# Prompt attention of a hybrid decoder step: two heads of each key group per unit, one fp32 copy of the probabilities, row scaling on GpSimd

## The reference

```python
def nsa_attend(q, gts, q_pos, k_cmp, v_cmp, k_sel, v_sel, k_win, v_win, win_pos, rel_bias):
    qs = q * (HEAD_DIM ** -0.5)
    ...
    lg = jnp.einsum('bqghd,bngd->bghqn', qs, k_cmp) + tab[t5_bucket(d_cmp)].transpose(2, 3, 0, 1)
    p_cmp = masked_softmax(lg, m_cmp)
    o_cmp = jnp.einsum('bghqn,bngd->bqghd', p_cmp.astype(v_cmp.dtype), v_cmp)
    ...
    o_sel = jnp.einsum('bghqnk,bgqnkd->bqghd', p_sel.reshape(shp).astype(vs.dtype), vs)
    ...
    o_win = jnp.einsum('bghqw,bwgd->bqghd', p_win.astype(v_win.dtype), v_win)
    g = jax.nn.sigmoid(gts.astype(jnp.float32)).astype(q.dtype)[..., None]
    return g[:, :, 0] * o_cmp + g[:, :, 1] * o_sel + g[:, :, 2] * o_win
```

## Time and profile before

| | |
|---|---|
| median of 3 runs | 1977.09 us (1969.35 to 1984.14) |
| span of the profiled execution | 1956.9 us |
| what lies between its span and the median | 20.2 us |
| prompt attention, first transpose to last fold | 616.65 us |
| TensorE, VectorE, ScalarE, GpSimd busy in that stretch | 551.09, 491.77, 448.30, 0.00 us |

### The profile page before, as it was taken

How to read it: one execution, slowest core, us unless ns; L and a number is a source line. 1 busy time by engine, 2 the same in 40 slices (tenths; PEclk the granted TensorE clock), 3 DMA queues, 4 the chain that set the end, 5 groups by cost and what they waited for, 6 DMA issues and landing times.

```text
span 1956.9 us, 25523 instructions
## 1 busy us (share of the span) xinstructions
PE 1734.6 (89%) x9736; PEld 1455.2 (74%) x9736; DVE 922.1 (47%) x1784; ACT 734.6 (38%) x1443; POOL 96.0 (5%) x156
## 2 busy tenths in 40 slices
PE   5798999999999998996889988998898758879996
PEld 1387999999999997664777777777677535568883
DVE  0443222221221222345887887787787645533321
ACT  0132111111111112435677777777777523232110
POOL 1003000000000002100000000000000000000000
PEclk9899999999999999988899999999999969889998
DMA  6419533233233225621002100100100164433320
GB/s 235 142 44 160 166 88 77 75 76 87 66 76 87 66 54 206 213 82 52 12 22 50 33 22 23 44 22 22 33 23 22 55 221 155 135 107 111 108 73 17
DMA packets 166924, 164.66 MB, mean 84 GB/s; under 512 B 48322, under 2 KB 143170, under 8 KB 162507
## 3 DMA queue, kind: packets, MB, share of 16 engines
q1 hardware_dynamic: 152100, 93.49, 17.6%
q0 software_dynamic: 14704, 69.53, 11.3%
HBM read 131.32 MB, written 35.83 MB: 85 GB/s over the span
## 4 chain that ended last, share of the span: by engine, by line
PE 75%; DVE 8%; ACT 6%; DMA 5%; issue 4%; SPq 0%; DVEq 0%; POOL 0%; ACTq 0%
PE PS L749 28%; PE PS L1034 9%; PE PS L786 4%; PE PS L877 4%; PE PS L865 3%; DVE ptl L1555 3%; PE PS L837 3%; PE PS L838 3%; ACT pth L1187 2%; PE PS L878 2%; PE PS L1000 2%; DMA adaw<-in_ada_w 2%; PE PS L967 2%; PE PS L885 2%; DMA wr<-in_w_in 2%
## 5 line engine op out<-in xcount | busy, mean ns | idle before, releaser
L749 PE MATMUL PS<-hhi,wh 128*128 128x352 f32 x1152 | 251.4, 326 | 10.5 <-DVE wl L1386 6.9
L749 PE MATMUL PS<-hhi,wl 128*128 128x352 f32 x1152 | 249.5, 324 | 0.0
L749 PE MATMUL PS<-hlo,wh 128*128 128x352 f32 x1152 | 249.3, 325 | 0.0
L1187 ACT ACTIVATE pth<-PS 128x512 fp32r<-128x512 f32 x296 | 176.9, 597 | 140.8 <-PE PS L865 139.0
L1510 DVE TENSOR_REDUCE nm<-PS 128x1 f32<-128x640 f32 (+7 forms) x256 | 180.4, 705 | 77.7 <-PE PS L845 75.5
L1555 DVE TENSOR_TENSOR ptl<-PS,pth 128x512 fp32r<-128x512 f32 x296 | 203.5, 688 | 26.3 <-ACT pth L1187 19.3
L749 PEld LDWEIGHTS PS<-hhi,wh 128*128 128x128 f32 x1152 | 197.1, 190 | 11.7 <-issue 11.2
L749 PEld LDWEIGHTS PS<-hhi,wl 128*128 128x128 f32 x1152 | 199.0, 189 | 0.0
L749 PEld LDWEIGHTS PS<-hlo,wh 128*128 128x128 f32 x1152 | 196.8, 189 | 0.0
L1170 ACT ACTIVATE pr<-PS,nm 128x640 f32<-128x640 f32 (+7 forms) x256 | 178.4, 697 | 30.4 <-DVE nm L1510 29.8
L865 PE MATMUL PS<-ident,pr 128*128 128x128 f32 x1056 | 158.9, 273 | 0.0
(11 more groups left out here) (297 smaller groups left out, 2844.0 us busy)
## 6 DMA issues: line engine op xcount, KB each, us to landing
wr<-in_w_in SPq DMA_DIRECT2D x32, 512.0 KB, 4.4
adaw<-in_ada_w SPq DMA_DIRECT2D x6, 2048.0 KB, 8.6
wr<-in_w_in SPq DMA_DIRECT2D x32, 256.0 KB, 3.5
qb<-q_stacked SPq DMA_DIRECT2D x32, 256.0 KB, 3.5
mr<-mixed SPq DMA_DIRECT2D x16, 512.0 KB, 3.8
mixed<-ych POOLq DMA_DIRECT2D x8, 528.0 KB, 3.3
z_attn_silu<-zab POOLq DMA_DIRECT2D x8, 528.0 KB, 3.0
xb<-in_x_prompt POOLq DMA_DIRECT2D x8, 512.0 KB, 3.8
```

Of the source, the lines that this page charges most:

```text
L749: ins = pe.matmul(PS[:, bank + c, 0:CH], a[kind % 2][:, k, :], b[:, k, c * CH:(c + 1) * CH], start=(k == 0 and b is hhi and a is wh), stop ...
L1187: act.activation(pth[tc % 2][:, :], PS[:, 4 + tc % 2, :], ACT.Copy).then_inc(pt_hi, 1)
```

## The change

A unit is now two heads of each key group (heads 2jp, 2jp+1 of both groups) for one query tile, still 4 heads. The transposed probabilities are copied once, in fp32, into one of six buffers (pt): even tiles by ScalarE, odd tiles by VectorE (copy_p). The products with the values are plain fp32, two for each tile: one for each key group, with 64 columns of stationary values and 256 of moving probabilities, one into partitions 0 to 63 of the output bank, the other into 64 to 127. The output bank alternates between 6 and 7; the fold (osb, reduce_o) is gone, and the split copies of the values as well. TensorE keeps the tiles in a list (held) and does the products of four or five tiles in a row. All four heads' rows are scaled on GpSimd. The query tensor is stored in the new order of heads; DMAs keep their number and sizes.

```diff
 
-ACT_A, ACT_B = {0, 1}, {0, 1}
+NPT5 = 6
...
-        osb = sb("osb", [P, 512], cx=c4)
-        zau = [sb(f"zau{i}", [P, 4, P], cx=c4) for i in range(2)]
-        mixs = [sb(f"mixs{i}", [P, 4, P], cx=c4) for i in range(2)]
+        pt = [sb(f"ptt{i}", [P, 4, P], cx=c4) for i in range(NPT5)]
+        zau = [sb(f"zau{i}", [P, 2, P], cx=c4) for i in range(2)]
+        mixs = [sb(f"mixs{i}", [P, 2, P], cx=c4) for i in range(2)]
...
         def unit(u):
-            return u // 16, u // 8 % 2, TILE_ORDER[u % 8]
+            return u // 8, TILE_ORDER[u % 8]
+
+        def head_of(u, h):
+            return 8 * (h // 2) + 2 * (u // 8) + h % 2
+
+        def pairs(t):
+            return t.rearrange("p (g j) -> p g j", g=NG)
 
         def tiles_of(w):
-            i = unit(w // 2)[2]
+            i = unit(w // 2)[1]
...
             cuts = [(n * q + 2) // 4 for q in range(5)]
             return [range(cuts[q], cuts[q + 1]) for q in range(4)]
+
+        def turned(c):
+
+            return (pt_dve if c % 2 else pt_act), c // 2 + 1
...
+
+            def scale(w):
+                k, r = keys_of(w)[0], w % 3
+                po.wait_ge(r_rdy, w + 1)
+                for h in range(4):
+                    ins = po.tensor_scalar(pr[r][:, h, 0:k], pr[r][:, h, 0:k], rg[:, r, h:h + 1], None, ALU.mult)
+                ins.then_inc(n_pool, 1)
+
             for b in range(NB):
                 if b == 1:
+                    for w in range(NI):
+                        scale(w)
                     po.wait_ge(r_ev, NU)
                     po.wait_ge(pv_mm, tile0[NI])
...
+                        pe.wait_ge(n_dve, w // 2 + 1)
                 if tc >= 2:
-                    pe.wait_ge(pt_hi, tc - 1)
-                    pe.wait_ge(pt_lo, tc - 1)
+                    pe.wait_ge(*turned(tc - 2))
                 for h in range(4):
                     cmp_ = w % 2 and t == tiles_of(w) - 1
...
             def values(w, t):
                 tc, u = tile0[w] + t, w // 2
-                g, hs, i = unit(u)
-                pe.wait_ge(pt_hi, tc + 1)
-                pe.wait_ge(pt_lo, tc + 1)
+                i = unit(u)[1]
+                pe.wait_ge(*turned(tc))
                 first, last = w % 2 == 0 and t == 0, w % 2 == 1 and t == tiles_of(w) - 1
-                if first and u:
-                    pe.wait_ge(o_ev, u)
-                v = vsx[:, t, g, :] if w % 2 == 0 else vcp[:, g, :] if last else vwx[:, max(0, i - 4) + t, g, :]
-                pe.matmul(PS[:, 6, :], v, pth[tc % 2][:, :], start=first, stop=False)
-                pe.matmul(PS[:, 6, :], v, ptl[tc % 2][:, :], start=False, stop=last).then_inc(pv_mm, 1)
-
-            def reduce_o(u):
-                g = unit(u)[0]
-                pe.wait_ge(o_ev, u + 1)
-                if u:
-                    pe.wait_ge(r_ev, u)
-                pe.matmul(PS[64 * g:64 * g + 64, 7, :], stack2[:, :], osb[:, :], start=True, stop=True).then_inc(r_mm, 1)
-
-            pe.wait_ge(vb_hi, 5)
-            pe.wait_ge(vb_lo, 3)
+                if first and u >= 2:
+                    pe.wait_ge(r_ev, u - 1)
+                for g in range(NG):
+                    if last:
+                        v = vcp[:, g, :]
+                    elif w % 2:
+                        v = kvt[:, max(0, i - 4) + t, C_VW + HD * g:C_VW + HD * g + HD]
+                    else:
+                        v = kvt[:, t, C_VS + HD * g:C_VS + HD * g + HD]
+                    ins = pe.matmul(PS[64 * g:64 * g + 64, 6 + u % 2, 0:2 * P], v, pt[tc % NPT5][:, 2 * g:2 * g + 2, :].rearrange("p j c -> p (j c)"), start=first, stop=last)
+                ins.then_inc(pv_mm, 1)
+
...
                 for h in range(4):
...
             for w in range(NI):
                 for h, part in enumerate(slots(w)):
-                    for t in part or [None]:
-                        if t in (None, part.start) and w + 2 < NI:
-                            scores(w + 2, h)
-                        if t is not None:
-                            turn_p(w, t)
-                        if t is not None:
-                            if behind:
-                                values(*behind)
-                            behind = (w, t)
-                    if h == 2 and w % 2 == 0 and w:
-                        reduce_o(w // 2 - 1)
-            values(*behind)
-            reduce_o(NU - 1)
+                    if w + 2 < NI:
+                        scores(w + 2, h)
+                    for t in part:
+                        turn_p(w, t)
+                        held.append((w, t))
+                    old = [x for x in held if x[0] < w - w % 2] if h == 2 else []
+                    go = max(len(old), len(held) - 1 if len(held) >= 5 else 0)
+                    for x in held[:go]:
+                        values(*x)
+                    held = held[go:]
+            for x in held:
+                values(*x)
...
 
-            def scale(w):
-                act.wait_ge(r_rdy, w + 1)
-                for h in sorted(ON_ACT[w % 2]):
-                    k, r = keys_of(w)[0], w % 3
-                    ins = act.activation(pr[r][:, h, 0:k], pr[r][:, h, 0:k], ACT.Copy, scale=rg[:, r, h:h + 1])
-                ins.then_inc(n_act, 1)
-
-            def high(w, t):
+            def copy_p(w, t):
                 tc = tile0[w] + t
                 act.wait_ge(t_mm, tc + 1)
-                if tc >= 2:
-                    act.wait_ge(pv_mm, tc - 1)
-                act.activation(pth[tc % 2][:, :], PS[:, 4 + tc % 2, :], ACT.Copy).then_inc(pt_hi, 1)
-
-            def sums(u):
-                act.wait_ge(pv_mm, tile0[2 * u + 2])
-                if u:
...
                 for h, part in enumerate(slots(w)):
-                    for t in part or [None]:
-                        if t in (None, part.start):
-                            if ahead:
-                                exps(*ahead)
-                            ahead = (w + 2, h) if w + 2 < NI else None
-                        if t is not None:
-                            high(w, t)
-                            if behind is not None:
-                                sums(behind)
-                                behind = None
-                    if w + 1 < NI and h == 2:
-                        scale(w + 1)
-                if w % 2:
-                    behind = w // 2
-            sums(NU - 1)
-            act.wait_ge(r_mm, NU)
+                    for t in part:
+                        if (tile0[w] + t) % 2 == 0:
+                            copy_p(w, t)
+                    if w + 2 < NI:
...
+                    dve.tensor_tensor(prc[r][:, :, 0:2 * i + 2], prc[r][:, :, 0:2 * i + 2], ext(rg[:, r, 4:8], (0, 2 * i + 2)), ALU.mult).then_inc(n_dve, 1)
+
+            def copy_p(w, t):
                 tc = tile0[w] + t
-                dve.wait_ge(pt_hi, tc + 1)
-                if tc >= 2:
-                    dve.wait_ge(pv_mm, tc - 1)
-                dve.tensor_tensor(ptl[tc % 2][:, :], PS[:, 4 + tc % 2, :], f32(pth[tc % 2][:, :]), ALU.subtract).then_inc(pt_lo, 1)
+                dve.wait_ge(t_mm, tc + 1)
+                if tc >= NPT5:
+                    dve.wait_ge(pv_mm, tc - NPT5 + 1)
+                dve.tensor_copy(pt[tc % NPT5][:, :, :], PS[:, 4 + tc % 2, :].rearrange("p (h c) -> p h c", h=4)).then_inc(pt_dve, 1)
 
             def gate_o(u):
-                g, hs, i = unit(u)
-                half = slice(64 * g, 64 * g + 64)
-                dve.wait_ge(r_mm, u + 1)
+                dve.wait_ge(pv_mm, tile0[2 * u + 2])
                 dve.wait_ge(za_ld[u % 2], 16 * (u // 2 + 1))
                 if u >= 2:
                     dve.wait_ge(mix_st[u % 2], 16 * (u // 2))
-                dve.tensor_tensor(mixs[u % 2][half, :, :], PS[half, 7, :].rearrange("p (j c) -> p j c", j=4), zau[u % 2][half, :, :], ALU.mult).then_inc(r_ev, 1)
+                dve.tensor_tensor(mixs[u % 2][:, :, :], PS[:, 6 + u % 2, 0:2 * P].rearrange("p (j c) -> p j c", j=2), zau[u % 2][:, :, :], ALU.mult).then_inc(r_ev, 1)
 
...
-                        if t is not None:
-                            if behind:
-                                low(*behind)
-                            behind = (w, t)
-                        if t in (None, part.start) and w + 2 < NI:
-                            maxima(w + 2, h)
-                    if w + 1 < NI:
-                        if h == 1:
-                            factors(w + 1)
-                        for hh in ((), (0, 1), (2, 3), ())[h]:
-                            scale(w + 1, hh)
+                    if w + 2 < NI:
+                        maxima(w + 2, h)
+                    for t in part:
+                        if (tile0[w] + t) % 2:
+                            copy_p(w, t)
+                    if w + 1 < NI and h == 1:
+                        factors(w + 1)
                     if h == 3 and w % 2 == 0 and w:
                         gate_o(w // 2 - 1)
-            low(*behind)
             gate_o(NU - 1)
```

152 lines of the change are left out of this document (63 added, 89 removed).

## The result

The kernel with the change takes 2076.19 us (median of 4 runs, 2061.09 to 2093.7), the kernel before 1973.22 in the same comparison (4 runs, 1967.61 to 1984.14). The ratio is 1.0555, with a 95% interval of 1.0497 to 1.0612: slower by 103 us, where 86 us less was forecast.

What follows compares the result with a forecast made beforehand. No engine was full in attention; TensorE waited 27.5 of 154.5 us a repeat, in lock step with the copies. Stage -92, GpSimd's delay +8, edges -2 made -86 us: 1977 to 1891, forecast 1890 us, range 1862 to 1955.

Steps and rivals of the forecast that it cites:

- the price of a column on GpSimd: Row scaling in attention: 1.1 ns a column, taken nearest to GpSimd's fills; 172 us in sum, hidden.
- My upper bound of 2.6 ns: GpSimd's scaling: reading, multiplying and writing each take a fill's time for a column.
- 4.9 us were needed and 4.7 free: Before 1024 keys: GpSimd's four rows need 4.9 us; TensorE's other work less VectorE's lag leaves 4.7.
- 2 us in a repeat, 8 in all: Attention stage: loss from GpSimd's scaling being 0.5 to 1 us late in a few short iterations.
- GpSimd sets the pace: Rival: GpSimd's scaling at 1.5 to 2.6 ns a column delays transposes; 1915 to 2010 us, middle 1940; chance 0.16.
- The value products: TensorE in attention: two fp32 halves run side by side, 0.43 us a tile, 31.8 us a repeat.
- two halves in series: Rival: a tile's two value products run one after another, 0.85 us instead of 0.43; 1991 us; chance 0.06.
- The change of shape: TensorE's switch of array shape around each block of value products: 0.3 us, 20 blocks and 6 us a repeat.
- mostly go: Attention: the 91 us of the products' waiting for ptl and pth should mostly vanish with the single copy.
- the waiting stays: Rival: waiting may only move from the products to the transposes; 1945 us; chance 0.12.
- The four short iterations: Four shortest iterations of a repeat: 25.4 us before, 16.5 of TensorE's work; taken as 21 after.
- The sum: Whole kernel: -92 us attention stage, +8 GpSimd's delay, -2 edges, making -86 us.

Runs made afterwards that it cites:

- The probe: The kernel before with GpSimd instructions on scratch tiles during the large projection, four forms at three sizes; multiplying 1024 columns by a per-row scalar took 2851 ns.
- two-and-two kernel: The changed kernel with row scaling taken off GpSimd, heads 0 and 1 on ScalarE, 2 and 3 on VectorE, in slot 1: 1883.62 us, ratio 0.9575.
- Three kernels with the same instructions on TensorE: The changed kernel (2076.19 us), it with factors made in slot 0 instead of 1 (1957.43 us), and it with GpSimd's scaling as a product of two tensors (1914.31 us).
- factors in slot 0, two and two: The two-and-two kernel with the factors and VectorE's scaled rows moved to slot 0 from slot 1: 1921.46 us, ratio 0.9781.
- groups apart: The two-and-two kernel with a block's value products ordered as all of key group 0 first, then all of group 1: 1958.35 us, ratio 0.9936.
- smaller blocks: The two-and-two kernel with value products one tile behind their transposes, 219 blocks instead of 79: 1920.26 us, ratio 0.9806; with three of six buffers 1924.7 us.
- three-engine split: The changed kernel with scaling of head 0 on ScalarE, 1 and 2 on VectorE, 3 on GpSimd: 1889.65 us, ratio 0.9595.
- one row to three: The two-and-two kernel with scaling of one row on ScalarE and three on VectorE instead: 1898.59 us, ratio 0.9651.
- product form: The changed kernel with GpSimd's scaling written as a product of two tensors, the factor repeated along the row: 1914.31 us, ratio 0.9765.

## Why the prediction was wrong

**The step that failed** is the price of a column on GpSimd: 1.1 ns and 0.09 us an instruction, against 2.5 ns and some 0.3 us measured. I took it because the fills were the nearest rows. They are nearest in the engine, not in the operation. The probe shows that copies do run near that rate (1.04 ns) and that multiplication doesn't (1.85 to 2.8). My upper bound of 2.6 ns, reading, multiplying and writing at a fill's time each, was close to the true value (11.0 us by it for four rows of 1024 keys, 11.3 measured), but the three fill times are not shown to be what it is made of; the argument that a fill has its own start-up in it said nothing on arithmetic.

From this price all else follows as the sum had it. In front of the 1024 keys 4.9 us were needed and 4.7 free. Measured, 11.3 us are needed. The free time came out near: TensorE idled 5.5 us of them, so it had 5.8. "2 us in a repeat, 8 in all" became 26 us of added waiting in a repeat.

**The rival "GpSimd sets the pace"** was the right one, and I gave it 0.16. The rule from the Trainium skill (GPSIMD Engine Reference, Performance versus the Vector engine) pointed the right way: by its 2.6 cycles an element, at the 1.2 GHz that it counts with, I estimate 2.2 ns a column for a product of two inputs. This case's traces show less, 1.85 (1893 ns for 1024 columns in the stage, 1.90 us in the probe). The form that the kernel uses is dearer than the page's figure, 2.8. That should have moved the chance, since no row spoke against it for arithmetic.

**The rival's own price was too low as well**: at 2.6 ns I had 2010 us, and it is 2076. What it left out is the clock. In the stage the granted clock was 1.00 before and in the two-and-two kernel, and 0.89 after. It falls around the waits: in the iteration with the 5.5 us wait it is 0.75. By that, the same records take 18 us more in a repeat, 72 in the stage. Three kernels with the same instructions on TensorE show the two going together: with 129.7, 50.3 and 26.2 us of this waiting the clock is 0.89, 0.96 and 0.99. How much clock a given wait costs is not settled by the runs: some waits of 2.8 us after the change are followed by no fall, and a repeat with none above 1.1 us (factors in slot 0, two and two) has one.

**The value products**, the term that I had called the decisive one, came out right: 0.43 us a tile foretold, 0.43 measured. The "two halves in series" can be had on purpose (groups apart) only in part: it costs 0.70 us a tile and not 0.85, since in a block of five tiles four of the sixteen steps still serve both halves, and with the scaling on ScalarE and VectorE even that order is no slower than the kernel before (1958.35 us).

**The change of shape** was put at 0.3 us a block; the starts show 0.24, and smaller blocks cost 0.22 each.

**The copies.** The waiting for them that was to "mostly go" is gone, and "the waiting stays" is refuted: with the scaling out of GpSimd the transposes waited 9.4 us in the stage for anything. The four short iterations take 21.9 us in the two-and-two kernel, where I took 21 between 16.5 and 25.4. VectorE and ScalarE, 332 and 277 us busy without any scaling, were forecast at 330 and 255.

**The sum.** Without GpSimd's 8 us I had 1882; the kernel without scaling takes 1871.03 and the two-and-two kernel 1883.62, beside kernels before of 1966.26 rather than 1977. Against those the gains are 95 and 83 us; 94 were forecast. So one term of the sum was wrong by some 190 us (8 foretold, about 200 measured between GpSimd's scaling and none), and it alone put the result outside the range of 1862 to 1955.

**The best version** is the change with the scaling left on ScalarE and VectorE, two rows each: ratio 0.9575, faster than both kernels. The three-engine split (0.9595) and one row to three (0.9651) can't be told apart from it.

**Still open**: why GpSimd's form with one scalar for each partition is slower than its product of two tensors, and which waits of TensorE bring the clock down. A share of rows for GpSimd in the product form wasn't tried, nor the product form with factors in slot 0.

## What to carry to other kernels

Price an operation on an engine by a row of the same kind of operation on that engine; where there is none, the bound is as likely as the near row, and a measured rate from elsewhere that speaks against the move deserves more than a small chance. Compare the delay that a moved step adds between producer and consumer with the work that stands there, not its busy time with the stage: an engine at 56% held up the whole kernel because its four rows run in series. And count a wait of TensorE of some microseconds twice, once for its length and once for the lower clock at which the work around it then runs.

## What the hardware showed that I had not expected

- On GpSimd a product of two tensors, one of them a repeated factor, is faster than the multiplication by a scalar: 1893 against 2845 ns for 128x1024 fp32, and a copy takes 1069.
- GpSimd and VectorE, both working in SBUF, slow each other: 492 to 698 ns for VectorE's scaling of a row (mean 528 columns), 2845 to 3404 for GpSimd's of 1024. A mean of three instructions can hide it: 2.21, 1.90 and 2.75 us for the same product.
- With waits of TensorE of up to 5.5 us, 51 times in 718, the mean granted clock was 0.89 instead of 1.00 and the same records took 14% longer (146.1 against 128.1 us in a repeat).
- Ten fp32 products of 64 stationary and 256 moving columns take 2.31 us when they alternate between the two halves of the output's partitions, and 3.65 when all of one half come first; then only four of the steps serve both halves.
